# MLA heads 0 to 14: attention weights transposed by VectorE in 32x32 blocks and 16 on-chip DMAs per head, in place of TensorE transposes

## What is computed

```python
s = (jnp.einsum('bqhd,bkhd->bhqk', qn, k_nope)
     + jnp.einsum('bqhr,bkr->bhqk', qr, k_rope)).astype(jnp.float32) * scale
s = jnp.where(causal, s, NEG_INF)
p = jax.nn.softmax(s, axis=-1).astype(v.dtype)
return jnp.einsum('bhqk,bkhd->bqhd', p, v)
```

## Time and profile before

| | us |
|---|---|
| median of 3 runs | 2143.83 |
| lowest, highest | 2143.45, 2144.72 |
| span of the profiled execution | 2142.7 |
| TensorE busy in it | 2130.9 |
| VectorE, ScalarE busy | 1425.0, 972.7 |

### The profile page before, as it was taken

How to read it: one execution, slowest core, us unless ns; L and a number is a source line. 1 busy time by engine, 2 the same in 40 slices (tenths; PEclk the granted TensorE clock), 3 DMA queues, 4 the chain that set the end, 5 groups by cost and what they waited for, 6 DMA issues and landing times. The chain is left out here.

```text
span 2142.7 us, 30716 instructions
## 1 busy us (share of the span) xinstructions
PE 2130.9 (99%) x10146; PEld 1783.4 (83%) x10146; DVE 1425.0 (67%) x2637; ACT 972.7 (45%) x1906; POOL 145.8 (7%) x167
## 2 busy tenths in 40 slices
PE   9999999999999999999999999999999999999999
PEld 7888888888888888888888888888888888888887
DVE  6676667676823568888888733686767686769432
ACT  6444444444432435555555633544454455456221
POOL 0100000000210010000000112200000000003000
PEclk9999999999999999999999999999999999999999
DMA  7322322334543623333333643532333333234642
GB/s 227 94 58 81 83 83 83 83 83 148 182 118 78 193 75 89 88 88 88 88 88 88 203 131 105 174 107 60 111 91 100 88 96 104 78 110 152 201 123 69
DMA packets 376882, 235.11 MB, mean 110 GB/s; under 512 B 9472, under 2 KB 349696, under 8 KB 376832
## 3 DMA queue, kind: packets, MB, share of 16 engines
q1 hardware_dynamic: 376832, 234.47, 38.2%
HBM read 210.33 MB, written 24.12 MB: 109 GB/s over the span
## 5 line engine op out<-in xcount | busy, mean ns | idle before, releaser
L625 PE MATMUL pp<-act_hi,w_hi 128*128 128x512 f32 x2304 | 907.2, 394 | 3.2 <-DVE w_lo L599 2.2
L627 PE MATMUL pp<-act_hi,w_lo 128*128 128x512 f32 x2304 | 898.6, 390 | 0.0
L626 PE MATMUL pp<-act_lo,w_hi 128*128 128x512 f32 x2304 | 898.5, 390 | 0.0
L599 DVE TENSOR_TENSOR w_lo<-raw,w_hi 128x512 fp32r<-128x512 f32 x680 | 457.5, 704 | 248.8 <-ACT w_hi L591 247.6
L591 ACT ACTIVATE w_hi<-raw 128x512 fp32r<-128x512 f32 (+1 forms) x684 | 399.0, 625 | 348.3 <-PE pp L627 180.7
L627 PEld LDWEIGHTS pp<-act_hi,w_lo 128*128 128x128 f32 x2304 | 433.1, 188 | 92.1
L625 PEld LDWEIGHTS pp<-act_hi,w_hi 128*128 128x128 f32 x2304 | 433.6, 188 | 91.5 <-DVE w_lo L599 3.2
L626 PEld LDWEIGHTS pp<-act_lo,w_hi 128*128 128x128 f32 x2304 | 433.9, 188 | 84.7 <-issue 0.2
L1885 ACT ACTIVATE s_prob<-ps,s_minus 128x256 f32<-128x256 f32 x96 | 44.7, 471 | 104.9 <-DVE s_minus L1964 97.8
L1227 ACT ACTIVATE prob<-ps,minus,q_scale 128x512 f32<-128x512 f32 (+1 forms) x64 | 39.0, 615 | 79.3 <-DVE minus L1293 79.3
L625 PE MATMUL ps<-act_hi,w_hi 128*128 128x512 f32 x176 | 69.3, 394 | 0.0
(11 more groups left out here) (416 smaller groups left out, 2839.5 us busy)
## 6 DMA issues: line engine op xcount, KB each, us to landing
raw<-w_in SPq DMA_DIRECT2D x48, 1024.0 KB, 5.9
raw<-swa_w_in SPq DMA_DIRECT2D x36, 1024.0 KB, 5.6
raw<-mla_w_in SPq DMA_DIRECT2D x23, 1024.0 KB, 5.8
raw<-mla_w_out SPq DMA_DIRECT2D x16, 1024.0 KB, 6.7
raw<-swa_w_out SPq DMA_DIRECT2D x16, 1024.0 KB, 6.3
raw<-w_out SPq DMA_DIRECT2D x16, 1024.0 KB, 7.3
x_feature_major<-xT SPq DMA_DIRECT2D x8, 1024.0 KB, 8.5
y_whole<-y_feature_major SPq DMA_DIRECT2D x7, 1024.0 KB, 6.8
```

Of the source, the lines that this page charges most:

```text
L599: q.eng.tensor_tensor(dst, raw_piece(tile, p), high, ALU.subtract).then_inc(s_lo, tile.ups(p))
L625: q.eng.matmul(psum[:, :], wh, ah, start=start and n == 0, stop=False)
L626: q.eng.matmul(psum[:, :], wh, al, start=False, stop=False)
L627: last = q.eng.matmul(psum[:, :], wl, ah, start=False, stop=stop and n == PIECE // P - 1)
```

## The change

For the bodies with projection and attention (1 to 15) the transposes on TensorE go. VectorE transposes the 32x32 blocks of `prob` into a new buffer `turned` with six instructions (`turn_blocks`, step turned, directly behind norm0). A 128x128 block is then transposed within each 32x32 block, but the blocks still have to move between groups of 32 partitions. 16 DMAs of 32 partitions by 320 columns, issued by SyncE, do that into `gathered` (`gather_dmas`). ScalarE rounds all of it to `pT_hi` in one instruction (turned_hi, behind tanh) and VectorE subtracts in one (turned_lo, behind the last `w_lo` of the next gate tile). pv waits for turned_lo (even bodies) or v_lo3 (odd ones). Queries stand in `pT` in another order now, so pv reads and writes strips, and y puts them back in order. Body 16 keeps its TensorE transposes. `dynamic_dma_scratch_size=1024` makes room for the two buffers; two small memsets are added at the start.

```diff
@@ attention_dmas (SyncE)
+            def gather(i):
+                q.eng.wait_ge(*q.at("V.turned", body=i, phase=phase))
+                gather_dmas(q, SLOTS)
...
                 for k in range(tiles):
                     load_tile(q.eng, Tile(phase, i, k, odd))
+                    if phase == "mla" and k == 0 and store:
+                        gather(i - 1)
@@ new helpers
+        def turn_blocks(q, weights, step):
+            for j, first, n in TURN_PIECES:
+                slot = SLOT_OF[j] + first - j
+                out_ = turned[:, 0:QUADS * SLOTS].rearrange("p (g n) -> p g n", g=QUADS)[:, :, slot * Q32:(slot + n) * Q32]
+                m = q.eng.transpose(out_.rearrange("p g (b n) -> p b g n", n=Q32), blocks_of(weights, j, first, n))
+            m.then_inc(*q.did(step))
...
+        def gather_dmas(q, run):
+            for a in range(QUADS):
+                for k in range(QUADS):
+                    q.eng.dma_start(gathered[k * Q32:(k + 1) * Q32, a * run:(a + 1) * run],
+                                    turned[a * Q32:(a + 1) * Q32, k * run:(k + 1) * run]).then_inc(s_turned, 16)
@@ mla_T (TensorE)
             def turn(b, free):
-                if attn:
+                if not proj:
...
-                q.eng.wait_ge(*q.at("V.v_lo3" if odd else "V.pt_lo0"))
+                q.eng.wait_ge(*q.at("V.v_lo3" if odd else "V.turned_lo" if proj else "V.pt_lo0"))
...
+                    if proj:
+                        m = products(q, queries_of(po, j), (v_hi[:, j, cols], v_lo[:, j, cols]),
+                                     (keys_of(pT_hi, j), keys_of(pT_lo, j)), j == 0, j == NB - 1)
@@ mla_A (ScalarE)
                 q.eng.activation(th[:, :], gate, ACT.Tanh, scale=0.5).then_inc(*q.did("tanh"))
+            if proj and attn:
+                q.eng.wait_ge(s_turned, lin(0, 16 * QUADS * QUADS, i))
+                copy_hi(q, by_quads(pT_hi)[:, :, Q32:], gathered_blocks(), "turned_hi")
@@ mla_V (VectorE)
+                else:
+                    q.eng.wait_ge(*q.at("V.norm0"))
+                    turn_blocks(q, prob, "turned")
             for p in range(PIECES):
                 up_lo(p)
...
             next_lo(3)
+            if proj and attn:
+                q.eng.wait_ge(*q.at("A.turned_hi"))
+                sub_lo(q, by_quads(pT_lo)[:, :, Q32:], gathered_blocks(), by_quads(pT_hi)[:, :, Q32:], "turned_lo")
```

More of the change, by code:

```diff
@@ L42 @@
 PIECE = 512
+Q32 = 32
+QUADS = P // Q32
+GATHER = 2 * 7 * P
+SLOTS = 10 * Q32
+SLOT_OF = [1, 5, 8, 0]
+TURN_PIECES = ((0, 0, 2), (0, 2, 2), (1, 1, 1), (1, 2, 2), (2, 2, 2), (3, 3, 1))
+PT_GROUP = SLOTS + Q32
 PHASES = {"load": (1, 0, 0), "in": (1, 1, 9), "mla": (H1 + 1, H1, 2), "out1": (KC // 2 - 1, KC // 2, 2),
@@ L104 @@
         "T": "s3 s2 s1 s0 t3 t2 t1 t0 values pv".split(),
-        "A": "exp3 exp2 exp1 exp0 pt_hi3 pt_hi2 pt_hi1 pt_hi0 tanh qa_hi qb_hi v_hi0 v_hi1 v_hi2 v_hi3 kn_hi qn_hi".split(),
-        "V": ("mask3 top3 minus3 mask2 top2 mask1 top1 mask0 top0 minus inv3 norm3 inv0 norm2 norm1 norm0 pt_lo3 "
-              "pt_lo2 pt_lo1 pt_lo0 gate v_lo0 v_lo1 v_lo2 v_lo3 q_cos q_sin0 q_sin1 q_sin2 q_sin3 qr kn_ev qa_lo "
+        "A": "exp3 exp2 exp1 exp0 pt_hi3 pt_hi2 pt_hi1 pt_hi0 tanh turned_hi qa_hi qb_hi v_hi0 v_hi1 v_hi2 v_hi3 kn_hi qn_hi".split(),
+        "V": ("mask3 top3 minus3 mask2 top2 mask1 top1 mask0 top0 minus inv3 norm3 inv0 norm2 norm1 norm0 turned pt_lo3 "
+              "pt_lo2 pt_lo1 pt_lo0 gate turned_lo v_lo0 v_lo1 v_lo2 v_lo3 q_cos q_sin0 q_sin1 q_sin2 q_sin3 qr kn_ev qa_lo "
               "qb_lo kn_lo qn_lo y silu").split(),
@@ L366, in sb @@
             return scope.enter_context(nc.sbuf_tensor(name, shape, dt))
+        turned, gathered = sb("turned", [P, GATHER]), sb("gathered", [P, GATHER])
+        sb("below", [P, 256])
         with ExitStack() as scope:
@@ L749, in attention_dmas @@
                 load_tile(q.eng, Tile(f"out{n}", 0, k))
+                if phase == "mla" and k == 0:
+                    gather(units - 1)
             for part in range(3):
@@ L1072, in in_V @@
                     q.eng.memset(pT_hi[:, hidden].bitcast(F32), 0.0).then_inc(*q.did("z1"))
+                    q.eng.memset(by_quads(pT_hi)[:, :, 0:Q32].bitcast(F32), 0.0)
+                    q.eng.memset(by_quads(pT_lo)[:, :, 0:Q32].bitcast(F32), 0.0)
                     q.eng.memset(pT_lo[:, hidden].bitcast(F32), 0.0).then_inc(*q.did("z2"))
@@ L1196, in mla_T @@
                     first = min(j, 2) * P
-                    m = products(q, po[:, first:S], (v_hi[:, j, cols], v_lo[:, j, cols]),
-                                 (pT_hi[:, PT_STEP * j + first:PT_STEP * j + S], pT_lo[:, PT_STEP * j + first:PT_STEP * j + S]), j == 0, j == NB - 1)
+                    if proj:
+                        m = products(q, queries_of(po, j), (v_hi[:, j, cols], v_lo[:, j, cols]),
+                                     (keys_of(pT_hi, j), keys_of(pT_lo, j)), j == 0, j == NB - 1)
+                    else:
+                        m = products(q, po[:, first:S], (v_hi[:, j, cols], v_lo[:, j, cols]),
+                                     (pT_hi[:, PT_STEP * j + first:PT_STEP * j + S], pT_lo[:, PT_STEP * j + first:PT_STEP * j + S]), j == 0, j == NB - 1)
                 m.then_inc(*q.did("pv", rest=not proj))
```

28 lines of the change are left out of this document (26 added, 2 removed).

## The result

| | before | after |
|---|---|---|
| median of the runs, us | 2143.64 | 2196.66 |
| lowest, highest | 2143.45, 2144.72 | 2195.49, 2197.93 |
| span of the profiled execution | 2142.7 | 2195.2 |

The changed kernel takes 1.0247 times as long, with a 95% interval of 1.0235 to 1.0259: 53 us more. The direction was forecast, the size was not: 2157.5 stands 39 us too low, and the range ended at 2185.

The account below looks back on a forecast made before the run. TensorE bounds the kernel, with VectorE's chain last in even bodies. Odd bodies -8.8, body 1's wait -1.3, even bodies +23.8: +13.7 on the 2142.7 span, 2156.4, plus 1.1 for the median: 2157.5 us, range 2139 to 2185.

Parts of the forecast that it names:

- The bound: TensorE busy for 99% of the span; in even bodies VectorE's chain from q_cos to qn_lo already ends last.
- the path through transposes, SyncE, ScalarE and VectorE: After norm0: transposes 2.25 us, 16 issues, landing 2.0, turned_hi 1.26, turned_lo 1.50; even bodies' q_cos 3.4 us late.
- the place of the wait: Even bodies: TensorE waits behind pv for VectorE (q_stack, qn_lo), nearly 5 us in each of seven.
- The pv strips: pv products in strips of 128, 96 or 64 columns, costed at nothing; a fifth more would be under 6 us.
- the wait for q_stack_b: Even bodies, TensorE behind pv: a wait of about 3.9 us in one piece, before the next head's rope scores.
- turned_lo is just in time: Even bodies: turned_lo ends at 234.2, pv would start at 234.9, so pv does not wait.
- The gathers have fixed addresses, so 0.44: SyncE's 16 issues stand 0.44 us apart, the last starting 6.6 after the first; bounds 0.37 to 0.57.
- Rival 3: TensorE's clock falls in the new even-body waits: 7 x 2.7 = +19 us, 2176; chance 0.18.
- seldom come together: High end: q_cos 8 us late gives 2190; since this and the clock case seldom coincide, the range ends at 2185.
- Hides it, with about 2 us to spare.: Odd bodies: v_lo ends near 261.5, pv needs it at 263.8, so the DMAs are hidden and 1.10 us is gained.
- The side: Whole kernel: slower 0.70, same 0.13, faster 0.17; about 4.3 us counted as a distinguishable change.
- Rival 1: Gathers land before ScalarE reaches them, needing issues about 0.25 apart; only odd bodies gain, 2136; chance 0.17.

Follow-up runs that it names:

- run 3: Kernel before, without the ten TensorE transposes of each of heads 0 to 14, copies taking whatever stands in PSUM: 2129.68 us, ratio 0.9932.
- Runs 8 and 10: Kernel before plus unused VectorE transposes and 16 unused DMAs per head: first 128 partitions by 80 columns, 2153.81 us; second 32 by 320 written to DRAM, 2151.41 us.
- run 1: Changed kernel plus 16 unread 512-column matmuls on TensorE behind pv in even bodies, filling its wait: 2183.03 us, ratio 1.0184.
- run 2: Changed kernel with 8 gather DMAs of 32 partitions by 640 columns instead of 16, same bytes, blocks in wrong places: 2143.48 us, ratio 1.000.
- run 6: Kernel before with new transposes in odd bodies only, turned_hi behind v_hi, turned_lo behind v_lo, pv waiting for turned_lo: 2138.32 us, ratio 0.9975.

## Why the prediction was off, step by step

**What held.** The bound (TensorE, and VectorE's chain at the end of even bodies), the path through transposes, SyncE, ScalarE and VectorE, and the place of the wait. turned_hi took 1.27 (1.26 forecast), turned_lo 1.49 (1.50), the landing 1.9 (2.0), ten transposes on TensorE 1.1 (run 3). The pv strips cost nothing: their starts lie as far apart as before. The loads of the up-projection went out 20.2 us behind the body's first score, 10.3 later than before (7.5 forecast), and no TensorE wait for them appears. That the wait for q_stack_b came at 4.08 us (3.9 forecast) is no proof of the landing time: pv itself waits for turned_lo, and q_cos starts right behind turned_lo, so from there on both engines are late together. The 2.3 us that q_cos came later than forecast stand ahead of pv: 0.7 is the slack that the prediction left there (turned_lo at 234.2, pv at 234.9), the other 1.6 are the seven waits of 1.6 us, where it had "turned_lo is just in time".

**The failed step: the spacing of the issues.** "The gathers have fixed addresses, so 0.44", with bounds of 0.37 and 0.57. It was 0.63, outside both bounds: 15 x 0.19 = +2.8 us per even body. My rows were loads from DRAM, and I carried their price to DMAs between two places in SBUF, a kind of which no row of the kernel before exists. Runs 8 and 10 show that just this makes the difference. The fixed or computed address, which I took for the cause of 0.44 against 0.55, says nothing here. Where no row shows the kind of transfer, the upper bound should have been a wide one. The transposes gave back 0.44 (1.81 instead of 2.25), so q_cos came 2.3 us later than forecast: 16 of the 39 us.

The Trainium skill's 311 ns for a 128x128 transpose on VectorE (VectorE: DVE Perf Modes, The three transpose paths) is for bf16, and would have given 3.1; the trace has 0.18 us a block for float32 in these shapes. The measurement decides, and it lies below my estimate as well. The rule of the Trainium skill that sends such a block to TensorE agrees with the runs: 0.11 us a block there and no DMAs, against 0.18 on VectorE for 32x32 blocks that still have to be moved.

**The clock.** Rival 3 had the right mechanism, and 2.7 us per wait where run 1 shows 1.9 (2.5 in the scores, less the 0.6 for qn_lo that they cover), and I set it at 0.18 as if it stood beside the forecast. It did not: my own forecast contained seven waits of 3.9 us, longer than the 1.70 at the start of the span, behind which products of 512 columns started 0.43 apart. "No later row shows such a wait" was no argument against it, because no later wait was as long. It belonged in the sum: 13.6 of the 39 us. It also set the end of the range: I held it at 2185 because a late q_cos and the low clock "seldom come together". They came together: each wait that a late q_cos made had the low clock behind it. On top of the 2157.5 the issues alone (+16) would have given 2174 and the clock alone (+13.6) 2171, both inside the range; the two together give 2187, outside it. The trace agrees here with the warning against idle gaps that the prediction named from the Trainium skill (TensorE: Matmul & The Clock Gate, Why this matters for your kernels).

**The odd body.** "Hides it, with about 2 us to spare." The spare was 2.3 (263.8 less 261.5), and the DMAs came 2.3 later. The odd body of the changed kernel shows it used up. ScalarE's timeline:

```profile
275.77 1.27 ACT L651 ACTIVATE pT_hi<-gathered 128x1280 fp32r<-128x1280 f32 x1 [5.28 <-DMA gathered<-turned]
276.95 1.55 ACT L651 ACTIVATE v_hi<-ps,rstd_tok 128x256 fp32r<-128x256 f32 x4
```

VectorE's:

```profile
277.07 1.49 DVE L655 TENSOR_TENSOR pT_lo<-gathered,pT_hi 128x1280 fp32r<-128x1280 f32 x1 [6.71 <-ACT pT_hi L651]
278.48 1.65 DVE L1417 SCALAR_TENSOR_TENSOR v_lo<-ps,rstd_tok,v_hi 128x256 fp32r<-128x256 f32 x4
```

TensorE's:

```profile
280.27 0.50 PE L659 MATMUL po<-pT_hi,v_hi 128*128 128x512 f32 x1
```

v_lo ends at about 280.1, and pv starts at 280.27, which is 0.24 later than its place in a row of matmuls, and pv takes 2.05 instead of 1.93 from there to the next head's first score: 0.3 to 0.4 us a pair. In body 1 the wait for v_lo is 2.8 us, and about 1.5 us of that body behind it run at 1.2 GHz, which costs 0.8: together about the 3.5 by which it was missed. In run 2, where the DMAs are in time, body 1 lasts 24.57, 2.6 less than before (2.4 forecast). The two ends stay open: 0.6 ahead of body 1's first score (131.0 before, 131.7 after) and 1.8 from body 16's on (1604.5 and 1606.3). The change touches neither but for two memsets and the two buffers. Over the traces of the ten runs the second stretch lies anywhere between 1604.4 and 1607.3, so its part may be no more than that spread.

**The sum again**, per pair of bodies: +2.3 forecast, +2.3 for the issues less the transposes, +1.9 for the clock, and +0.5 that is left for the odd body, of which 0.3 to 0.4 are seen in its rows: 7.0 measured. Seven pairs make +49; body 1 (+1.1) and the ends (+2.4) bring it to +52.5.

**The side.** Slower was right, and for the right reason. Rival 1 (hidden) needed issues 0.25 apart; they were 0.63. What the removal alone is worth is 14 us (run 3), of which run 6 gets 6.

## What to carry to other kernels

Price a queue of small DMAs by its issues, from a row of the same kind of transfer: 16 issues between two places in SBUF cost 10 us here, and halving their number with the same bytes (run 2, whose blocks are not the right ones) took back 53 us. Where a forecast contains a TensorE wait of some microseconds, put the low clock behind it into the sum, not among the rivals. And when data comes late on an in-order engine, look first at what stands behind the wait without needing it: moving turned_hi and turned_lo behind the copies of the values turned 2146.7 into 2138.3. The same in even bodies, with q_cos ahead of turned_lo, was not tried.

## What was not expected of the hardware

- An issue on SyncE's queue takes 0.59 us (0.63 from one to the next) for a DMA from SBUF to SBUF, be it 32 or 128 partitions, 40 or 80 KB; 0.42 (0.46) for one from SBUF to DRAM. On ScalarE's queue eight of the first kind take 5.31, 0.66 each. The Trainium skill (DMA: Bandwidth & Descriptors, Anatomy of one DMA) splits a DMA's time, for the GpSimd path, into about 50 ns in the sequencer, a small and variable part for descriptors, and for most of it the time until the write is confirmed. On SyncE's queue, another path, the runs show 0.4 to 0.6 us of the queue's own, and here that decided the result. The same page of the Trainium skill calls that confirmation heaviest for DRAM. No run shows it by itself; from the start of the issue to the landing 40 KB took 1.6 us to DRAM and 1.9 within SBUF.
- VectorE's transpose of 32x32 blocks in float32: 1.81 us for 1280 columns in six instructions. The subtraction turned_lo takes 1.49 for as many columns in one.
- Behind seven waits of 4.1 us the clock was at 1.2 GHz each time, for 4.9 to 6.4 us, and for 3.4 behind one of 2.8. Behind waits of 1.2 to 1.4 us followed by one of 0.6 (run 2) it fell in three heads and not in four, in one and the same execution. Why was not tried.
